# The RWKV scan: group norm of y moved to ScalarE, VectorE's order in a chunk changed, the samples' columns loaded first

## The chip, the cores and the metric

The program runs on one core of a Trainium2 chip (trn2). The metric is the device time of one execution in microseconds (us), lower is better. The kernel before takes 2999.13 us (median of 3 runs, 2998.64 to 3001.56). All data is fp32.

## What is computed

The whole program is one inference step of a 2-layer decoder trunk: an RWKV-7 layer and an attention layer, each followed by a squared-ReLU MLP, for one prompt of 1024 tokens and 8 samples of one token. The change lies in the RWKV-7 mixer, in its recurrence and in the norm of its output:

```python
def wkv7_step(state, inp):
    r_t, w_t, k_t, v_t, a_t, b_t = inp
    sa = jnp.einsum('bhij,bhj->bhi', state, a_t)
    state = (state * w_t[:, :, None, :] + sa[..., None] * b_t[:, :, None, :]
             + v_t[..., None] * k_t[:, :, None, :])
    y = jnp.einsum('bhij,bhj->bhi', state, r_t)
    return state, y
...
    state, y = lax.scan(wkv7_step, wkv_prev.astype(f32), xs)
    y = jnp.moveaxis(y, 0, 1)
    mu = jnp.mean(y, axis=-1, keepdims=True)
    var = jnp.mean(jnp.square(y - mu), axis=-1, keepdims=True)
    y = ((y - mu) * lax.rsqrt(var + LNX_EPS) * lnx_g.astype(f32).reshape(H, N)
         + lnx_b.astype(f32).reshape(H, N))
```

There are 16 heads of 64 channels. The mean and the variance are taken over the 64 channels of a head, for each token. The prompt starts from a zero state; the 8 samples have one step each, from a given state.

## The kernel before

The program is a row of stages, and between them all engines meet. The scan (`stage_scan`) follows the stage that makes its inputs (`stage_kvr`) and stands in front of the output projection with `rw_wo`. It handles the prompt in 16 chunks (NCH) of 64 tokens (C). Within a chunk the recurrence is a set of small matrix products, each made for 8 pairs of heads (DB = 8 blocks of 128 channels). Four chunks are one body of the loop (BODY = 4); the last four are written out.

One chunk, with the names of the PSUM tiles (the profile calls pSA c_pA):

- TensorE: `pU` takes 8 pairs of matmuls with the state S and 8 with the values V (the latter need the masked grams G). Then half of the grams of the next chunk into pB and pK, `pSA` from U, `pD` and `pY` with V and S, a wait for SA, then `pD` (the change of the state) and `pY` (the output), the other half of the next chunk's grams, and in `turn` four transposes of the y of three chunks ago (Y_LAG = 3) into pT.
- VectorE and ScalarE each copy one half of U, and one half of SA, out of PSUM into block-diagonal tiles. VectorE also masks the grams (`masked`, two halves, each two operations) and sums S from pD and the decayed state Sd.
- GpSimd makes the diagonal of the next chunk's decays (`diagonal`), which the grams need, and Sd, the decayed state.
- The norm of y runs beside it, some chunks late. Before the change: VectorE reduces y to sums and scales them (`mean`), GpSimd subtracts the mean and squares, VectorE reduces the squares (`variance`), ScalarE takes the root (`root`), VectorE the reciprocal (`inverse`), GpSimd multiplies y by it (`normalise`).
- VectorE works besides on the 8 samples (`Samples.step`): nine operations a chunk on 128x256 elements, in three parts of three, L2326 to L2328, L2329 to L2331 and L2332 to L2334. All but the two reduces read two tensors in SBUF. Their inputs come as columns (`Samples.load`), are turned by TensorE (`turn`) and evicted by ScalarE (`spread`), written to memory and loaded again by rows; the samples' state of 2 MB is loaded behind that.

The order on each engine is written out by hand, in `work(c, k, i, last)` of each engine's block; semaphores tie the engines together. VectorE's order in a chunk before is: copy of U, `inverse`, sample part 0, masks of half 0 for the next chunk, copy of SA, sample part 1, `variance`, sum into S, sample part 2, `mean`, masks of half 1.

Of the kernel before, what the change touches and what calls it, by code (L numbers as in the profile page):

```python
# [22 lines left out]
HD = 64  # L23
# [3 lines left out]
Y_LAG = 3  # L27
# [2356 lines left out]
def stage_scan(net):  # L2384
# [15 lines left out]
    with ExitStack() as ctx:  # L2400
# [16 lines left out]
        ym, yv, yi = (sb(n, [128, Q * 2]) for n in ("ym", "yv", "yi"))  # L2417
# [10 lines left out]
        s_ym, s_yc, s_ysq, s_yv, s_yr, s_yi, s_yn = sem("ym"), sem("yc"), sem("ysq"), sem("yv"), sem("yr"), sem("yi"), sem("yn")  # L2428
# [28 lines left out]
        each = lambda x: x.unsqueeze(2).to_broadcast([128, Q * 2, HD])  # L2457
# [39 lines left out]
        @block.gpsimd  # L2497
        def _(pool):
            pool.memset(BK[:, 0, 0], 0.0).then_inc(s_zeroP, 1)
            pool.memset(BK[:, 1], 0.0).then_inc(s_zeroP, 1)  # L2500
            pool.wait_ge(s_eye, 2)

            def work(c, k, i, last):
                s, cc = k // 2, k % 2
                decay = net.pend[:, :, bass.ds(c, 1)]
                pool.wait_ge(s_S, c + 1)
                pool.wait_ge(s_D, c + 1)
                if not last:
                    diagonal(c + 1, (k + 1) % BODY)
                pool.tensor_tensor(Sd[:], S[:], decay.to_broadcast([128, DB, 128]), ALU.mult).then_inc(s_dS, 1)  # L2510
                normalise(c, k)

            def normalise(c, k, full=True):
                y = heads(Y[:, (k - 3) % BODY])
                pool.wait_ge(s_yi, c + 1)
                pool.tensor_tensor(y, y, each(yi[:]), ALU.mult).then_inc(s_yn, 1)
                if not full:
                    return
                y = heads(Y[:, (k - 1) % BODY])
                pool.wait_ge(s_ym, c + 1)  # L2520
# [12 lines left out]
            for k in range(Y_LAG):  # L2533
                normalise(NCH + k, k, k == 0)

        @block.tensor
        def _(pe):
# [54 lines left out]
            def turn(c, k):  # L2592
                pe.wait_ge(s_yn, c + 2)
# [27 lines left out]
        def _(act):  # L2621
            for s in range(2):
                smp.load(act, (2 * s, 2 * s + 1))
                act.wait_ge(s_zeroV, s + 1)
                values(act, s, s)
            smp.spread(act, (pT, pY, pU, pSA, pD))

            def work(c, k, i, last):
# [3 lines left out]
                ins.then_inc(s_Ua, 1)  # L2632
                act.wait_ge(s_SA, c + 1)
# [3 lines left out]
                root(c)  # L2637
# [18 lines left out]
            def root(c):  # L2656
                act.wait_ge(s_yv, c + 1)
                act.activation(yv[:], yv[:], ACT.Sqrt).then_inc(s_yr, 1)
# [10 lines left out]
            for k in range(Y_LAG):  # L2669
                if k < 2:  # L2670
                    root(NCH + k)
# [10 lines left out]
        def _(dve):  # L2682
# [9 lines left out]
            for n, buf in enumerate((Y, ysq, Yt)):  # L2692
                dve.memset(buf[:], 0.0).then_inc(s_ydv, 1)
            dve.memset(yv[:], 1.0).then_inc(s_ydv, 1)
# [6 lines left out]
            for x in (s_yc, s_ysq, s_yn, s_yr, s_yTe, smp.s_dv, s_Yev, s_Ua, s_Ud, s_Sa, s_Sd, s_D):  # L2701
# [8 lines left out]
            def work(c, k, i, last):  # L2710
# [5 lines left out]
                inverse(c)  # L2716
# [10 lines left out]
                smp.step(dve, c, 1)  # L2727
                variance(c)
# [11 lines left out]
            def mean(c, k, made, n=2):  # L2740
                dve.wait_ge(s_Yev, made + 1)
                dve.wait_ge(s_yc, c + 1)
                dve.tensor_reduce(ym[:], heads(Y[:, (k - 1) % BODY]), AX, ALU.add).then_inc(s_ydv, 1)
                dve.wait_ge(s_ydv, 4 + c * 2 + n)
                dve.tensor_scalar(ym[:], ym[:], 1.0 / HD, None, ALU.mult).then_inc(s_ym, 1)

            def variance(c, n=1):
                dve.wait_ge(s_ysq, c + 1)
                dve.tensor_reduce(yv[:], ysq[:], AX, ALU.add).then_inc(s_ydv, 1)
                dve.wait_ge(s_ydv, 4 + c * 2 + n)  # L2750
                dve.tensor_scalar(yv[:], yv[:], 1.0 / HD, LNX_EPS, ALU.mult, ALU.add).then_inc(s_yv, 1)

            def inverse(c):
# [7 lines left out]
            for k in range(Y_LAG):  # L2761
                inverse(NCH + k)
                if k == 0:
                    mean(NCH, 0, NCH, 1)
                if k < 2:
                    dve.wait_ge(s_yi, NCH + k + 1)
                    variance(NCH + k, 2 - k)
# [514 lines left out]
```

## Time and profile before

| | us |
|---|---|
| median of 3 runs | 2999.13 |
| profiled execution | 2994.69 |
| its span | 2992.9 |
| PE busy in the span | 2689.9 |
| DVE busy | 1277.1 |
| ACT busy | 944.0 |
| POOL busy | 590.9 |

PE is TensorE, PEld its weight loads, DVE VectorE, ACT ScalarE, POOL GpSimd, SP SyncE. A row of the timeline tells the start in us, the duration, the engine, the line, what is written from what, the shape, and in brackets how long the engine stood idle before it and what ended that. PEclk is the clock granted to TensorE as a share of its full 2.4 GHz, so 0.50 is 1.2 GHz. Over the whole program PE is the busiest engine; within the scan this is a matter of its own, which the rows show.

### The profile page before, as it was taken

To read this page: it belongs to the slowest core of one execution; us is meant where nothing else is said; L and a number is where in the kernel's file an instruction comes from. 1 tells how busy PE (TensorE), PEld (TensorE's weight loads), DVE (VectorE), ACT (ScalarE), POOL (GpSimd) and SP (SyncE) were. 2 spreads that over 40 slices of the span, in tenths; PEclk is the share of its full clock that TensorE was granted. 3 is DMA by queue.
4 is the path that set the end of the run, shared out by engine and by line. 5 is a ranking of instruction groups with operands and counts; after the bars stand their busy time and mean duration, and the time that the engine had idled before them with its cause. 6 is when DMAs were issued, how large, how long until landed. Compare 5 with 4: busy or idle time off the path is not lost. (4 is left out here: it accounts for less than half of the span.)

```text
span 2992.9 us, 46796 instructions
## 1 busy us (share of the span) xinstructions
PE 2689.9 (90%) x19528; PEld 2531.1 (85%) x19528; DVE 1277.1 (43%) x2250; ACT 944.0 (32%) x1809; POOL 590.9 (20%) x357
## 2 busy tenths in 40 slices
PE   4879878958886899999999999898899999999998
PEld 3648768947775789999999999777799999999998
DVE  5236776338886742121121235466563222121223
ACT  4337623312213442121120234356543122131221
POOL 1011111113344002112112230210201222221230
PEclk7989989989997899999999999999999999999999
DMA  8866659684465412222222231411111111111121
GB/s 317 305 225 205 207 183 272 202 183 106 101 139 192 130 50 86 92 71 85 92 85 85 71 97 53 121 28 47 55 60 36 50 44 49 50 43 50 49 65 57
DMA packets 379486, 331.87 MB, mean 111 GB/s; under 512 B 109863, under 2 KB 349163, under 8 KB 372221
## 3 DMA queue, kind: packets, MB, share of 16 engines
q1 hardware_dynamic: 349180, 287.17, 32.1%
q10 hardware_dynamic: 24384, 21.87, 2.5%
q0 software_dynamic: 5728, 20.06, 1.8%
q8 instruction: 145, 2.38, 0.3%
q14 instruction: 49, 0.39, 0.0%
HBM read 248.92 MB, written 78.78 MB: 109 GB/s over the span
## 5 line engine op out<-in xcount | busy, mean ns | idle before, releaser
L524 POOL TENSOR_TENSOR wL<-raw,wH 128x1024 fp32r<-128x1024 f32 x120 | 288.1, 2401 | 1297.0 <-ACT wH L648 1297.0
L545 PE MATMUL t_acc<-oneH,wH 128*128 128x344 f32 x1488 | 482.6, 324 | 12.3 <-DVE oneL L892 6.3
L547 PE MATMUL t_acc<-oneH,wL 128*128 128x344 f32 x1488 | 477.6, 321 | 0.0
L546 PE MATMUL t_acc<-oneL,wH 128*128 128x344 f32 x1488 | 477.2, 321 | 0.0
L545 PE MATMUL t_acc<-twoH,wH 128*128 128x344 f32 x1392 | 449.0, 323 | 7.0 <-DVE twoL L867 4.8
L547 PE MATMUL t_acc<-twoH,wL 128*128 128x344 f32 x1392 | 445.5, 320 | 0.0
L546 PE MATMUL t_acc<-twoL,wH 128*128 128x344 f32 x1392 | 445.1, 320 | 0.0
L817 DVE SCALAR_TENSOR_TENSOR X<-t_acc,mod,X 128x344 f32<-128x344 f32 (+1 forms) x240 | 137.4, 572 | 611.4 <-PE t_acc L547 590.2
L897 DVE TENSOR_TENSOR t_g<-t_g 128x344 f32<-128x344 f32 x192 | 99.3, 517 | 553.3 <-ACT t_g L668 553.3
L545 PEld LDWEIGHTS t_acc<-oneH,wH 128*128 128x128 f32 x1488 | 281.4, 189 | 26.4 <-issue 10.1
L648 ACT ACTIVATE wH<-raw 128x1024 fp32r<-128x1024 f32 x120 | 126.7, 1056 | 507.6 <-PE t_acc L547 507.6
L546 PEld LDWEIGHTS t_acc<-oneL,wH 128*128 128x128 f32 x1488 | 281.9, 189 | 0.6
L547 PEld LDWEIGHTS t_acc<-oneH,wL 128*128 128x128 f32 x1488 | 281.5, 189 | 0.0
L545 PEld LDWEIGHTS t_acc<-twoH,wH 128*128 128x128 f32 x1392 | 262.3, 188 | 20.1 <-issue 11.2
L546 PEld LDWEIGHTS t_acc<-twoL,wH 128*128 128x128 f32 x1392 | 262.6, 189 | 0.1
L547 PEld LDWEIGHTS t_acc<-twoH,wL 128*128 128x128 f32 x1392 | 262.3, 188 | 0.0
L668 ACT ACTIVATE t_g<-t_acc 128x344 f32<-128x344 f32 x192 | 87.7, 457 | 507.8 <-PE t_acc L547 507.8
L1962 PE MATMUL kvr_acc<-hxH,kvr_wH 128*128 128x344 f32 x480 | 161.8, 337 | 20.8 <-POOL kvr_wL L1844 17.5
L1963 PE MATMUL kvr_acc<-hxL,kvr_wH 128*128 128x344 f32 x480 | 156.1, 325 | 0.0
L1964 PE MATMUL kvr_acc<-hxH,kvr_wL 128*128 128x344 f32 x480 | 155.9, 325 | 0.0
L545 PE MATMUL t_acc<-twoH,oneH 128*128 128x344 f32 x336 | 113.5, 338 | 31.4 <-DVE twoL L892 30.7
L1844 POOL TENSOR_TENSOR kvr_wL<-kvr_wraw,kvr_wH 128x1024 fp32r<-128x1024 f32 x24 | 63.3, 2636 | 334.1 <-ACT kvr_wH L2000 334.1
(481 smaller groups left out, 5039.4 us busy)
## 6 DMA issues: line engine op xcount, KB each, us to landing
raw<-in_mlp_down SPq DMA_DIRECT2D x64, 512.0 KB, 3.8
raw<-in_mlp_up SPq DMA_DIRECT2D x62, 512.0 KB, 4.2
ada_ring<-in_ada_w SPq DMA_DIRECT2D x24, 1024.0 KB, 8.7
shared<-in_ada_w SPq DMA_DIRECT2D x24, 1024.0 KB, 6.2
kvrb_hx<-hx_saved ACTq DMA_DIRECT2D x16, 516.5 KB, 3.7
kvr_work<-scr_L SPq DMA_DIRECT2D x16, 516.0 KB, 5.1
X<-x_saved SPq DMA_DIRECT2D x6, 1376.0 KB, 7.5
raw<-in_at_wqkv SPq DMA_DIRECT2D x12, 512.0 KB, 4.0
```

What stands on the lines that cost most here:

```text
L524: pool.tensor_tensor(low, raw_of(w), high.bitcast(F32), ALU.subtract).then_inc(s_low, 1)
L545: pe.matmul(out, high[:, k, :], h[:, k, third[t]], start=(k == 0), stop=False)
L546: pe.matmul(out, high[:, k, :], l[:, k, third[t]], start=False, stop=False)
L547: return pe.matmul(out, low[:, k, :], h[:, k, third[t]], start=False, stop=(k == DB - 1))
L648: act.activation(place(kind, p)[0], raw_of(w), ACT.Copy).then_inc(s_high, 1)
L668: act.activation(gsq[:, i % 3, :], acc[u % 4][:, 0:TT], ACT.Relu).then_inc(s_relu, 1)
L817: ins = dve.scalar_tensor_tensor(out=x, in0=acc[u % 4][:, 0:z - a], scalar=gate[:, m, 0:1], in1=x, op0=ALU.mult, op1=ALU.add)
L897: dve.tensor_tensor(x, x, x, ALU.mult).then_inc(s_g, 1)
L1844: pool.tensor_tensor(wL[:, p % 2], raw[:, p % 2], wH[:, p % 2].bitcast(F32), ALU.subtract).then_inc(s_low, 1)
L1962: pe.matmul(out, wH[:, s, b, :], net.HH[:, b, t], start=(b == 0), stop=False)
L1963: pe.matmul(out, wH[:, s, b, :], net.HL[:, b, t], start=False, stop=False)
L1964: ins = pe.matmul(out, wL[:, s, b, :], net.HH[:, b, t], start=False, stop=(b == DB - 1))
```

## The change

Three things.

The norm of y leaves GpSimd. ScalarE squares y less its mean by heads, eight instructions of 128x64 with an accumulated sum (`squares`), and scales by heads, eight of 128x64 with a scale and a bias per partition (`normalise`). VectorE loses the reduce of the squares and gains one product of 128x8 (`nm`). ym and yv get a place per chunk of the body.

VectorE's order in a chunk becomes: copy of U, sample part 0, copy of SA, `variance`, masks of half 0, `inverse`, sum into S, sample part 1, `mean`, masks of half 1, sample part 2.

ScalarE issues all four loads of the samples' columns, and the samples' values, in front of its loads of V.

```diff
@@ gpsimd @@
                 pool.tensor_tensor(Sd[:], S[:], decay.to_broadcast([128, DB, 128]), ALU.mult).then_inc(s_dS, 1)
-                normalise(c, k)
-
-            def normalise(c, k, full=True):
-                y = heads(Y[:, (k - 3) % BODY])
-                pool.wait_ge(s_yi, c + 1)
-                pool.tensor_tensor(y, y, each(yi[:]), ALU.mult).then_inc(s_yn, 1)
-                if not full:
-                    return
-                y = heads(Y[:, (k - 1) % BODY])
-                pool.wait_ge(s_ym, c + 1)
-                pool.tensor_tensor(y, y, each(ym[:]), ALU.subtract).then_inc(s_yc, 1)
-                pool.wait_ge(s_yc, c + 2)
-                pool.wait_ge(s_yv, c + 1)
-                pool.tensor_tensor(ysq[:], y, y, ALU.mult).then_inc(s_ysq, 1)
...
@@ tensor @@
             def turn(c, k):
-                pe.wait_ge(s_yn, c + 2)
+                pe.wait_ge(s_yn, c + 1)
...
@@ scalar @@
+            smp.load(act, range(4))
             for s in range(2):
-                smp.load(act, (2 * s, 2 * s + 1))
                 act.wait_ge(s_zeroV, s + 1)
                 values(act, s, s)
...
                 ins.then_inc(s_Ua, 1)
+                squares(c, k)
                 act.wait_ge(s_SA, c + 1)
                 for o, p in halves(0, SA, pSA):
                     ins = act.activation(o, p, ACT.Copy)
                 ins.then_inc(s_Sa, 1)
-                root(c)
+                root(c, k)
+                normalise(c, k)
                 act.wait_ge(s_Y, c + 1 + Y0)
                 act.activation(Y[:, k], pY[:], ACT.Copy).then_inc(s_Yev, 1)
                 turned(c, k, i)
...
+            def squares(c, k):
+
+                y = heads(Y[:, (k - 2) % BODY])
+                act.wait_ge(s_ym, c + 1)
+                act.wait_ge(s_ysq, c + 1)
+                for g in range(2 * Q):
+                    ins = act.activation(ysq[:, g, :], y[:, g, :], ACT.Square, bias=ym[:, (k - 1) % BODY, g:g + 1], accum_out=yv[:, k % BODY, g:g + 1])
+                ins.then_inc(s_ysq, 1)
+
+            def root(c, k):
                 act.wait_ge(s_yv, c + 1)
-                act.activation(yv[:], yv[:], ACT.Sqrt).then_inc(s_yr, 1)
+                act.activation(yv[:, k % BODY], yv[:, k % BODY], ACT.Sqrt).then_inc(s_yr, 1)
+
+            def normalise(c, k):
+                y = heads(Y[:, (k - 2) % BODY])
+                act.wait_ge(s_nm, c + 1)
+                for g in range(2 * Q):
+                    ins = act.activation(y[:, g, :], y[:, g, :], ACT.Identity, bias=nm[:, g:g + 1], scale=yi[:, g:g + 1])
+                ins.then_inc(s_yn, 1)
...
             for k in range(Y_LAG):
                 if k < 2:
-                    root(NCH + k)
+                    squares(NCH + k, k)
+                    root(NCH + k, k)
+                    normalise(NCH + k, k)
...
@@ vector @@
                 ins.then_inc(s_Ud, 1)
-                inverse(c)
                 dve.wait_ge(smp.s_S, 16)
                 dve.wait_ge(smp.s_vec, 96)
                 smp.step(dve, c, 0)
-                if not last:
-                    dve.wait_ge(s_Y, c + Y0)
-                    masked(c + 1, 1 - g, 0)
                 dve.wait_ge(s_SA, c + 1)
                 for o, p in halves(1, SA, pSA):
                     ins = dve.tensor_copy(o, p)
                 ins.then_inc(s_Sd, 1)
-                smp.step(dve, c, 1)
-                variance(c)
+                variance(c, k)
+                if not last:
+                    dve.wait_ge(s_Y, c + Y0)
+                    masked(c + 1, 1 - g, 0)
+                inverse(c, k)
                 dve.wait_ge(s_D, c + 2)
                 dve.wait_ge(s_dS, c + 1)
...
                 ins.then_inc(s_S, 1)
-                smp.step(dve, c, 2)
-                mean(c, k, c)
+                smp.step(dve, c, 1)
+                mean(c, k)
                 if not last:
                     masked(c + 1, 1 - g, 1)
...
+                smp.step(dve, c, 2)
+
+            def mean(c, k):
+                dve.wait_ge(s_Yev, c + 1)
+                dve.tensor_reduce(ym[:, k % BODY], heads(Y[:, (k - 1) % BODY]), AX, ALU.add).then_inc(s_ydv, 1)
+                dve.wait_ge(s_ydv, c + 5)
+                dve.tensor_scalar(ym[:, k % BODY], ym[:, k % BODY], -1.0 / HD, None, ALU.mult).then_inc(s_ym, 1)
+
+            def variance(c, k):
+                dve.wait_ge(s_ysq, c + 2)
+                dve.tensor_scalar(yv[:, k % BODY], yv[:, k % BODY], 1.0 / HD, LNX_EPS, ALU.mult, ALU.add).then_inc(s_yv, 1)
+
+            def inverse(c, k):
                 dve.wait_ge(s_yr, c + 1)
                 dve.wait_ge(s_yn, c + 1)
-                dve.reciprocal(yi[:], yv[:]).then_inc(s_yi, 1)
+                dve.reciprocal(yi[:], yv[:, k % BODY]).then_inc(s_yi, 1)
+                dve.wait_ge(s_yi, c + 1)
+                dve.tensor_tensor(nm[:], ym[:, (k - 1) % BODY], yi[:], ALU.mult).then_inc(s_nm, 1)
```

## Rows read from the trace of the kernel before

**Rows 1.** Busy time by windows, one stretch of the chunk loop: engine's busy us (instructions), clock, DMA.
```profile
720.00:904.00 184.00, 152.48 (x1932) 137.66 (x1930) 163.49 (x308) 39.27 (x86) 69.23 (x57) 1.00 0.55 118
```

**Rows 2.** Timeline of one chunk, VectorE.
```profile
744.27 0.68 DVE L2743 TENSOR_REDUCE c_ym<-c_Y 128x8 f32<-128x512 f32 x1
...
747.94 0.87 DVE L2714 COPY c_U<-c_pU 64x256 f32<-64x256 f32 x2 [1.20 <-PE c_pU L2540]
...
748.95 1.60 DVE L2326 TENSOR_TENSOR step_t<-step_S,step_vec 128x256 f32<-128x256 f32 x1
...
750.48 1.26 DVE L2327 TENSOR_TENSOR step_t<-step_vec 128x256 f32<-128x256 f32 x1
...
753.81 0.87 DVE L2725 COPY c_SA<-c_pA 64x256 f32<-64x256 f32 x2
...
756.89 1.73 DVE L2733 TENSOR_TENSOR c_S<-c_pD,c_Sd 64x256 f32<-64x256 f32 x4
```

**Rows 3.** The same timeline, TensorE, and ScalarE's copy of SA.
```profile
744.71 1.09 PE L2540 MATMUL c_pU<-c_S,c_ARI 128*64 128x128 f32 x16
...
746.79 1.09 PE L2540 MATMUL c_pU<-c_V,c_G 128*64 128x128 f32 x16 [0.99 <-DVE c_G L2708]
...
748.54 0.48 PE L2551 MATMUL c_pB<-c_ARI,c_BK 128*128 128x128 f32 x2 [0.65 <-POOL c_ARI L2528]
...
750.92 1.09 PE L2540 MATMUL c_pA<-c_U,c_Z 128*64 128x128 f32 x16
...
752.06 0.76 ACT L2635 ACTIVATE c_SA<-c_pA 64x256 f32<-64x256 f32 x2 [3.37 <-PE c_pA L2540]
...
754.83 1.09 PE L2540 MATMUL c_pD<-c_SA,c_G 128*64 128x128 f32 x16 [1.07 <-DVE c_SA L2725]
...
760.45 1.09 PE L2540 MATMUL c_pU<-c_S,c_ARI 128*64 128x128 f32 x16
```

**Rows 4.** The same timeline, GpSimd.
```profile
747.35 1.06 POOL L2528 TENSOR_TENSOR c_ARI<-c_eye,pend 128x512 f32<-128x512 f32 x1
...
748.36 1.91 POOL L2510 TENSOR_TENSOR c_Sd<-c_S,pend 128x1024 f32<-128x1024 f32 x1
...
750.23 1.23 POOL L2516 TENSOR_TENSOR c_Y<-c_Y,c_yi 128x512 f32<-128x512 f32 x1
```

**Rows 5.** Instructions by tile: duration ns min/median/max, first and last start.
```profile
L2329 DVE TENSOR_TENSOR step_S<-step_S,step_t x16: 424/426/426, 675.6 to 909.1; 128x256 f32 x12, 128x256 f32<-128x256 f32 x4
L2751 DVE TENSOR_SCALAR c_yv<-c_yv x18: 171/171/393, 677.6 to 922.8; 128x8 f32<-128x8 f32 x18
```

**Rows 6.** ScalarE: an accumulating one (attention, timeline), one with two pointers (groups).
```profile
1928.79 0.39 ACT L3110 ACTIVATE a_S<-a_S,a_nm 128x129 f32<-128x129 f32 x1
...
L683 ACT ACTIVATE shared<-shared,mod,gain 128x344 f32<-128x344 f32 x48 | 31.8, 663 | 15.5 <-DVE shared L852 15.5
```

**Rows 7.** Busy time by windows around two falls of the clock, and one PE row.
```profile
902.50:906.00 3.50, 1.59 (x26) 1.11 (x22) 2.26 (x5) 0.86 (x3) 3.42 (x3) 1.00 0.52 150
906.00:909.00 3.00, 2.96 (x28) 2.99 (x30) 2.95 (x6) 0.75 (x2) 1.54 (x2) 0.50 0.03 8
1026.50:1030.00 3.50, 0.23 (x2) 0.00 (x0) 3.46 (x6) 3.17 (x7) 0.80 (x1) 0.84 0.00 0
1030.00:1034.00 4.00, 2.33 (x7) 1.89 (x8) 2.74 (x6) 1.63 (x4) 0.00 (x0) 0.50 0.47 121
...
906.04 1.97 PE L2540 MATMUL c_pA<-c_U,c_Z 128*64 128x128 f32 x16 [1.06 <-DVE c_U L2714]
```

**Rows 8.** Timeline at the stage's head: first use of the columns and of the samples' state.
```profile
646.42 1.02 PE L2301 MATMUL c_pT<-const,step_cols 128*8 128x128 f32 x4 [21.51 <-DMA step_cols<-scr_Kt]
...
671.90 0.42 DVE L2326 TENSOR_TENSOR step_t<-step_S,step_vec 128x256 f32<-128x256 f32 x1 [7.81 <-DMA step_S<-in_state_wkv]
```

**Rows 9.** Timeline at the stage's end: issue of the prompt's state, last eviction of Yt.
```profile
915.40 2.17 ACTq L2668 DMA_DIRECT2D out_wkv_prompt<-c_St  x2
...
926.29 0.60 ACT L2651 ACTIVATE c_Yt<-c_pT 128x512 f32<-128x512 f32 x1 [0.99 <-PE c_pT L2596]
```

More of the change, by code:

```diff
@@ L2416, in stage_scan @@
         ysq = sb("ysq", [128, Q * 2, HD])
-        ym, yv, yi = (sb(n, [128, Q * 2]) for n in ("ym", "yv", "yi"))
+        ym, yv = (sb(n, [128, BODY, Q * 2]) for n in ("ym", "yv"))
+        yi, nm = (sb(n, [128, Q * 2]) for n in ("yi", "nm"))
         Yt = sb("Yt", [128, 2, DB, 2, C])
@@ L2427, in stage_scan @@
         s_dec, s_dS, s_eye = sem("dec"), sem("dS"), sem("eye")
-        s_ym, s_yc, s_ysq, s_yv, s_yr, s_yi, s_yn = sem("ym"), sem("yc"), sem("ysq"), sem("yv"), sem("yr"), sem("yi"), sem("yn")
+        s_ym, s_ysq, s_yv, s_yr, s_yi, s_nm, s_yn = sem("ym"), sem("ysq"), sem("yv"), sem("yr"), sem("yi"), sem("nm"), sem("yn")
         s_yT, s_yTe, s_ydv, s_yz = sem("yT"), sem("yTe"), sem("ydv"), sem("yz")
@@ L2456, in stage_scan @@
         heads = lambda y: y.rearrange("p q (a d) -> p (q a) d", a=2)
-        each = lambda x: x.unsqueeze(2).to_broadcast([128, Q * 2, HD])
         @block.sync
@@ L2532, in _ @@
             chunks(pool, work)
-            for k in range(Y_LAG):
-                normalise(NCH + k, k, k == 0)
         @block.tensor
@@ L2654, in turned @@
                     act.dma_start(net.sYc[:, :, bass.ds(c * C, 2 * C)].rearrange("b p t -> p b t"), Yt[:, slot].rearrange("p b c t -> p b (c t)")).then_inc(s_yst[slot], 16)
-            def root(c):
-                act.wait_ge(s_yv, c + 1)
-                act.activation(yv[:], yv[:], ACT.Sqrt).then_inc(s_yr, 1)
+            def squares(c, k):
[6 more added lines that the diff above has]
+            def root(c, k):
+                act.wait_ge(s_yv, c + 1)
+                act.activation(yv[:, k % BODY], yv[:, k % BODY], ACT.Sqrt).then_inc(s_yr, 1)
[5 more added lines that the diff above has]
+                ins.then_inc(s_yn, 1)
             act.wait_ge(s_yz, 1)
@@ L2691, in _ @@
                 dve.tensor_copy(eye[r], ident[r, r]).then_inc(s_eye, 1)
-            for n, buf in enumerate((Y, ysq, Yt)):
+            for buf in (Y, Yt, ym, yv):
                 dve.memset(buf[:], 0.0).then_inc(s_ydv, 1)
-            dve.memset(yv[:], 1.0).then_inc(s_ydv, 1)
             dve.wait_ge(s_ydv, 4)
@@ L2700, in _ @@
             dve.sem_inc(s_yst[1], 16)
-            for x in (s_yc, s_ysq, s_yn, s_yr, s_yTe, smp.s_dv, s_Yev, s_Ua, s_Ud, s_Sa, s_Sd, s_D):
+            for x in (s_ym, s_ysq, s_yn, s_yTe, smp.s_dv, s_Yev, s_Ua, s_Ud, s_Sa, s_Sd, s_D):
                 dve.sem_inc(x, 1)
@@ L2734, in work @@
                 ins.then_inc(s_S, 1)
-                smp.step(dve, c, 2)
-                mean(c, k, c)
+                smp.step(dve, c, 1)
+                mean(c, k)
                 if not last:
                     masked(c + 1, 1 - g, 1)
[L2740 to L2753, printed above, removed]
+                smp.step(dve, c, 2)
[8 more added lines that the diff above has]
+            def inverse(c, k):
                 dve.wait_ge(s_yr, c + 1)
                 dve.wait_ge(s_yn, c + 1)
-                dve.reciprocal(yi[:], yv[:]).then_inc(s_yi, 1)
+                dve.reciprocal(yi[:], yv[:, k % BODY]).then_inc(s_yi, 1)
+                dve.wait_ge(s_yi, c + 1)
+                dve.tensor_tensor(nm[:], ym[:, (k - 1) % BODY], yi[:], ALU.mult).then_inc(s_nm, 1)
             for half in range(2):
@@ L2760, in _ @@
             chunks(dve, work)
[L2761 to L2767, printed above, removed]
+            mean(NCH, 0)
+            for k in range(2):
+                variance(NCH + k, k)
+                inverse(NCH + k, k)
                 if k == 0:
```

## Prediction, made before the changed kernel was run

> **What bounds the kernel now.** I read the page first for the stage: the scan's sixteen chunks lie at about 660 to 914 us of the span. The view by windows comes next [rows 1]: over 184 us of the chunk loop VectorE (DVE) is busy 163.49 us, TensorE (PE) 152.48, GpSimd (POOL) 69.23 and ScalarE (ACT) 39.27, at a granted clock of 1.00, TensorE's upper level (2.4 GHz). The timeline of one chunk then shows who waits. The same matmuls onto pU start at 744.71 and 760.45 [rows 3], so a chunk takes 15.74 us. DVE stands idle for 1.20 us of that, before its copy of U [rows 2]. PE waits three times in a chunk: 0.99 us for DVE's masked grams, 0.65 for POOL's diagonal, 1.07 for DVE's copy of SA [rows 3]. DVE's order is the bound. Two things in it are waste. The copy of SA starts at 753.81 although ACT could start its half at 752.06, because the masks of the next chunk stand in front. And the first two sample steps take 1.60 and 1.26 us beside two POOL instructions that last over the same time [rows 2, 4], where the same form of instruction takes 0.43 us [rows 5]: each ends some 0.28 us after POOL's ends (748.36 + 1.91 = 750.27, against 750.55). So a DVE operation on two SBUF tensors stands still while a POOL one runs. That is 2.0 us in each chunk.
>
> **What the change does to a chunk, step by step.** I count from u, the start of the second group onto pU (746.79), which waits for the masks.
> Removed: POOL's three passes over Y, and with them POOL's lateness. POOL's diagonal and Sd no longer stand behind the mean, so PE's 0.65 goes. DVE loses a reduce of 128x512 (0.68, as the mean's) and gains one product of 128x8, 0.20 as the scalar operations with their gaps.
> Step a: from u, PE does its group, the grams and pA; SA could be copied at 752.06 - 746.79 - 0.65 = 4.6 us. By then DVE has done the third sample part, its copy of U and the first part, all undisturbed since POOL has long finished: 1.35 + 0.9 + 1.35 = 3.6 us. DVE waits there, 1.0 us.
> Step b: copy of SA 0.90 [rows 2], variance 0.20, masks of half 0, 1.6 (from the mean's start to pU it is 746.79 - 744.27 = 2.52, less the mean's 0.91 with its scalar operation), inverse with its product 0.45, sum into S 1.75 [rows 2]. PE's own work from the start of pA to the second group onto pD is 2.7 us without its wait (754.83 - 1.07 - 750.92 = 2.84, of which some is the tail of the last matmul). That makes pD start at u + 6.1 and end 1.1 later, before the sum into S at u + 7.7; it isn't late.
> Step c: the sum into S frees POOL at the same moment as it frees DVE's next part, which is now the second sample part: three products or sums on two SBUF tensors, each waiting for the last. POOL does diagonal (1.06) and Sd (1.91) at once [rows 4]. Counted from the end of that sum: the first DVE one gets through (0.43), the diagonal, started 0.1 to 0.3 behind, ends at about 1.33, the second ends at 1.61, Sd, delayed as the 1.23 us one in [rows 4], ends at 3.4, the third at 3.7. Undisturbed they would take 1.35. Even were they let through, the mean's scalar operation is stopped as well: one took 0.39 at the end of the stage, beside a pass of POOL's, 0.17 being usual [rows 5].
> Step d: mean and masks of half 1, 2.52, and the next u.
> Sum: 4.6 + 0.9 + 0.2 + 1.6 + 0.45 + 1.75 + 3.7 + 2.5 = 15.7 us. The chunk is as long as before. The 1.75 us won at SA, the 0.5 of the reduce and the 2.0 of contention come back as 2.35 of contention in front of the masks and as DVE's wait for SA.
> The masks of half 0 move behind the copy of SA; the grams of half 1, which wait for them, start 2.8 us after pD, the masks end 1.1 after it, so they hide. The wait for the root stands in front of the sum into S: ACT does the short root beside the masks of 1.6 us, and a table load in every fourth chunk fits there too. Were that cover gone it would cost up to the masks' 1.6 us in 4 of 16 chunks.
>
> **ScalarE.** It gets 8 squares with an accumulator and 8 scalings per chunk. The nearest row of the first kind is 128x129 in 0.39 us with its read [rows 6], these are 128x64; so 2.7 to 3.1 us per chunk. ACT is free from u + 1.9 (after its copy of U) and has to start on SA by 5.2, that is 3.3 us: they hide, by 0.2 to 0.6 us. The scalings, below 0.66 [rows 6] and I take 0.35 (280 columns fewer), are 2.8 us from u + 7.7, and Y's eviction behind them has until the next chunk. Nothing there is on the chain. Their price if squares cost 0.5 each is 0.7 us per chunk (11 us), kept for the range.
>
> **TensorE's clock.** PE ends its first group onto pU 6.7 us after pD's start (760.45 - 754.83 + 1.1) and waits for u at 15.7 - 6.1 = 9.6: 2.9 us idle in one piece in each chunk. Before, the pieces were 0.99, 0.65 and 1.07. The windows of [rows 7] show two falls: PE was busy for 0.23 of 3.5 us and the clock behind it was 0.50 (1.2 GHz); and in the last chunk it was busy for 1.59 of 3.5 us, in pieces with idles near 1 us between, and the 3 us after 906.0 had 0.50. There 16 matmuls took 1.97 us against 1.09. The first matmuls after the new idle piece are all on the chain (pU, grams, pA). A fall as the one at 906 lost 0.88 us on each of two groups, 1.7 in all, if it lies wholly behind the idle piece, and less where it begins in it. It need not come in each chunk: bounds 0 and 1.7 per chunk. I take 1.3, since the piece is nearer to the one of over 3 us that fell than to the 1.0 ones that didn't. Over 14 chunks + 18.2 us.
>
> **Ends of the stage.** Head: PE waited until 646.42 for the last of the samples' columns, and DVE 7.81 us for the samples' state, to 671.90 [rows 8]. ACT's loads now come in one row without its wait for the cleared V, so the columns land by about 640, and ACT's spread (held by its own issuing) starts 4 to 8 us earlier. The 2 MB state behind it shares the DMA engines, which are full there, with the other loads: I take 3 of these. In chunk 0 the copy of SA no longer follows the masks, 1.6, but the sample parts collide after it: 0.9 net. Together -3.7 (bounds -8 and 0).
> Tail: from the end of ACT's issue of the prompt's state (915.40 + 2.17) to the end of the last eviction of Yt (926.29 + 0.60) it took 9.3 us [rows 9], with the passes over Y on POOL. Now ACT does in that place twice 8 squares, root, wait for DVE and 8 scalings, 2 x (2.8 + 0.65 + 0.5 + 2.7) = 13.3, and 2.6 for the samples' root and columns, two evictions and the last transposes: 15.9. In front of it the last chunk's scalings hold Y's last eviction by 0.6. So +7.2 (bounds +4, +9). The stage behind starts only when these evictions have landed.
> Loop: 14 x (15.70 - 15.74) = -0.6.
> Sum: -3.7 + 7.2 - 0.6 + 18.2 = +21.1 us. On the profiled execution's 2994.7 us (span 2992.9 and 1.8 around it) that is 3015.8. That execution is 4.4 us under the median 2999.13 of the runs; the difference goes onto the median: **3020 us**.
>
> The Trainium skill (SBUF — State Buffer, Who interferes with whom) states what [rows 2, 4] show, that a DVE instruction with two SBUF inputs and a GpSimd one that reads SBUF exclude each other for a whole instruction. It speaks against this order: by it step 1 is put exactly where POOL starts. The sum above would be the same without it.
>
> **Rivals.**
> The clock holds: the idle piece of 2.9 us is shorter than the one of over 3 us behind which a row shows a fall, and the loop's own three pieces never brought one. Then +2.9: 3002 us. The Trainium skill (TensorE: Matmul & The Clock Gate, HAM oscillation — how this bites in real kernels) has falls begin with longer idle pieces than mine; by that rule this is the outcome. The fall at 906, after much shorter ones, speaks against it. Chance 0.17.
> The collision is smaller: POOL comes to its diagonal late enough, or loses to DVE each time. If only the scalar operation of the mean is stopped, a chunk is 15.7 - 1.2 = 14.5 us, the idle piece 1.7 and the clock mostly holds: -17.4 + 3.5, 2985 us. If nothing is stopped it is 15.7 - 2.35 = 13.35 us, and 14 x (13.35 - 15.74) + 3.5 = -30, 2969 us. For it: POOL's start behind a release is not shown for this pair. Against it: [rows 4], where POOL's instruction took the port ahead of a DVE one already issued. Chance 0.22.
> The clock's fall stretches: if it stays low through the whole of grams, pA and pD, up to 3 us per chunk, or the squares delay SA as well: +35 to +45, 3040 us. It decides where PE isn't busy enough in the low stretch to come back. Chance 0.11.
> My forecast has 0.50.
>
> **Numbers.** Differences under 0.2% (6 us) can't be told from no change. Slower: forecast and the stretched fall, 0.61, and a little of the rival at 3002: 0.63. Same: 0.15. Faster: 0.22. The range leaves out the undisturbed case and the far end: 2983 to 3036. The likeliest case's own range, with its bounds of clock and ends, is 3006 to 3031.
>
> **What would show it.** In the new profile: the second sample part's three instructions at 0.4, 1.2 and 2.0 us beside POOL's Sd; the copy of SA at once behind pA; PE idle 2.9 us before the second group onto pU, released by the last mask; granted clock about 0.85 to 0.9 over the loop; the chunk at 17 us; the last eviction of Yt some 16 us behind the issue of the prompt's state. Wrong it is if the masks of half 1 come less than 2 us after the sum into S, or if the clock stays at 1.00.

## The result, and the profile after

The changed kernel takes 3015.79 us (median of 5 runs, 3012.45 to 3023.66), the kernel before 2999.13 (5 runs, 2998.64 to 3001.56). The ratio is 1.0059, 95% interval 1.0043 to 1.0075: slower by 0.6%, by more than the runs' noise. The forecast was 3020 us.

| | before | after |
|---|---|---|
| median of 5 runs | 2999.13 | 3015.79 |
| profiled execution | 2994.69 | 3014.17 |
| its span | 2992.9 | 3012.3 |
| one chunk in the loop | 15.74 | 16.94 |
| PE / DVE / ACT / POOL busy in the span | 2689.9 / 1277.1 / 944.0 / 590.9 | 2712.1 / 1267.3 / 1040.8 / 540.5 |

The page of the kernel after, its first lines:

```profile
span 3012.3 us, 47136 instructions
## 1 busy us (share of the span) xinstructions
PE 2712.1 (90%) x19528; PEld 2554.3 (85%) x19528; DVE 1267.3 (42%) x2249; ACT 1040.8 (35%) x2241; POOL 540.5 (18%) x304
```

PE does the same 19528 matmuls in 22.2 us more: they did not grow, their clock fell. The view by windows of the kernel after, the stretch of [rows 1] (columns as there: PE, PEld, DVE, ACT, POOL busy, granted clock, DMA share, GB/s):

```profile
720.00:904.00 184.00, 156.07 (x1780) 144.65 (x1777) 149.37 (x286) 95.51 (x341) 35.51 (x22) 0.90 0.53 117
```

POOL went from 69.23 to 35.51 us and ACT from 39.27 to 95.51. DVE is down from 163.49 to 149.37, for the most part because the stretch holds fewer chunks: 163.49 us in 184 / 15.74 chunks are 14.0 us in each, 149.37 in 184 / 16.94 are 13.8. The granted clock was 1.00 and is 0.90. The timeline of one chunk after, its chain and what stands beside it:

```profile
747.47 1.40 PE L2524 MATMUL c_pU<-c_V,c_G 128*64 128x128 f32 x16 [2.54 <-DVE c_G L2711]
748.81 0.80 PE L2535 MATMUL c_pB<-c_ARI,c_BK 128*128 128x128 f32 x2
...
752.05 0.33 ACT L2648 ACTIVATE c_ysq<-c_Y,c_ym 128x64 f32<-128x64 f32 x1
...
752.50 1.09 PE L2524 MATMUL c_pA<-c_U,c_Z 128*64 128x128 f32 x16
...
753.64 0.76 ACT L2620 ACTIVATE c_SA<-c_pA 64x256 f32<-64x256 f32 x2 [1.17 <-PE c_pA L2524]
753.64 0.87 DVE L2724 COPY c_SA<-c_pA 64x256 f32<-64x256 f32 x2 [2.60 <-PE c_pA L2524]
...
756.53 1.72 DVE L2735 TENSOR_TENSOR c_S<-c_pD,c_Sd 64x256 f32<-64x256 f32 x4
756.64 2.76 ACT L2659 ACTIVATE c_Y<-c_Y,c_nm,c_yi 128x64 f32<-128x64 f32 x8 [1.69 <-DVE c_nm L2758]
...
758.28 0.43 DVE L2329 TENSOR_TENSOR step_S<-step_S,step_t 128x256 f32 x1
758.50 1.13 POOL L2514 TENSOR_TENSOR c_ARI<-c_eye,pend 128x512 f32<-128x512 f32 x1 [13.75 <-DVE c_S L2735]
...
758.75 1.17 DVE L2330 TENSOR_TENSOR step_t<-step_sa,step_vec 128x256 f32<-128x256 f32 x1
...
759.60 2.09 POOL L2510 TENSOR_TENSOR c_Sd<-c_S,pend 128x1024 f32<-128x1024 f32 x1
...
759.94 2.02 DVE L2331 TENSOR_TENSOR step_S<-step_S,step_t 128x256 f32 x1
...
761.89 0.67 DVE L2745 TENSOR_REDUCE c_ym<-c_Y 128x8 f32<-128x512 f32 x1
...
764.41 0.77 PE L2524 MATMUL c_pU<-c_V,c_G 128*64 128x128 f32 x10 [2.54 <-DVE c_G L2711]
```

The same matmuls start at 747.47 and at 764.41, 16.94 us apart. Three things are to be seen. The sum into S ends and lets go two engines at once: DVE's sample part 1 and POOL's diagonal with Sd. Three DVE instructions that take 0.4 us when left alone take 0.43, 1.17 and 2.02 beside them. PE runs out of work before the masks come and stands for 2.54 us. Behind that idle piece its matmuls are slow (1.40 us for the group onto pU, 0.80 for a pair of grams that takes 0.38 at the full clock), until pA is back at 1.09. So it is from the third chunk (696.67) to the fifteenth (900.12), 13 in all; in front of the second chunk PE stood even longer, and no fall followed:

```profile
681.36 1.09 PE L2524 MATMUL c_pU<-c_V,c_G 128*64 128x128 f32 x16 [3.03 <-DVE c_G L2711]
```

The granted clock from there to 684.90 was 1.00, and that chunk took 15.31 us (681.36 to 696.67).

Head and tail of the stage, from the same timeline: the spread of the samples' rows and the first sample step, and the end of the stage with the first instruction behind it:

```profile
645.98 0.59 ACT L2309 ACTIVATE step_rows<-c_pT 8x512 f32<-8x512 f32 x1 [35.24 <-PE c_pA L2301]
...
669.48 0.43 DVE L2326 TENSOR_TENSOR step_t<-step_S,step_vec 128x256 f32<-128x256 f32 x1 [5.15 <-DMA step_S<-in_state_wkv]
...
927.98 1.40 ACTq L2670 DMA_DIRECT2D out_wkv_prompt<-c_St  x2
...
933.15 2.76 ACT L2659 ACTIVATE c_Y<-c_Y,c_nm,c_yi 128x64 f32<-128x64 f32 x8 [0.47 <-DVE c_nm L2758]
...
940.68 2.76 ACT L2659 ACTIVATE c_Y<-c_Y,c_nm,c_yi 128x64 f32<-128x64 f32 x8 [0.47 <-DVE c_nm L2758]
...
945.25 0.60 ACT L2637 ACTIVATE c_Yt<-c_pT 128x512 f32<-128x512 f32 x1 [0.98 <-PE c_pT L2580]
...
950.30 1.06 ACT L648 ACTIVATE oneH<-raw 128x1024 fp32r<-128x1024 f32 x1 [4.46 <-PEq L122]
```

So the span's +19.4 us divide: the stage starts 0.7 later; from there to the second chunk's copy of U it takes 52.3 instead of 56.5 (-4.2); the fourteen chunks after that take 234.9 instead of 218.8 (+16.1); the issue of the prompt's state is 0.8 shorter (1.40 against 2.17, [rows 9]); from its end to the end of the last eviction it takes 16.5 instead of 9.3 (+7.2); the stages behind take 0.4 more.

### The profile page after: what moved, and what is told of

Same layout as the page of the kernel before. It is cut to its first block and busy times, and to the rows that moved or that the text cites. A ratio compares the mean times of both kernels' runs of the same rounds, so it can differ in the third digit from the quotient of the medians.

```text
span 3012.3 us, 47136 instructions
## 1 busy us (share of the span) xinstructions
PE 2712.1 (90%) x19528; PEld 2554.3 (85%) x19528; DVE 1267.3 (42%) x2249; ACT 1040.8 (35%) x2241; POOL 540.5 (18%) x304
```

## Experiments

The theory: a chunk is DVE's chain, with a collision in front of the masks that costs 2.35 us, and the idle piece of PE which that makes brings a fall of TensorE's clock. The rivals: the clock falls for another reason and costs nothing on the chain; the collision is not what sets the chunk; the norm's ACT work does. Where several ran together, they share the runs of the kernel before.

### The idle piece filled: e1_refill2 and e2_refill1

The changed kernel, whose first group onto pU is done three times in a row (e1) or twice (e2). The result is the same numbers, and nothing on DVE, ACT or POOL changes.

```diff
-                for b in range(DB):
-                    mm(pU, b, ARI[:, s, b, 0, cc, :], S[:, b, :], b < 2, False)
+                for again in range(3):
+                    for b in range(DB):
+                        mm(pU, b, ARI[:, s, b, 0, cc, :], S[:, b, :], b < 2, False)
```

> The changed kernel, with the first group of matmuls onto pU (8 pairs from S) made three times in a row instead of once; each time starts the sums anew, so the result is the same and only TensorE's idle piece in front of the second group is filled, by 2 x 0.88 of its 2.54 us. Theory (the fall of the clock after that piece costs 1.1 to 1.3 us per chunk): the granted clock stays at 1.00 over the loop, a chunk takes 15.7 us instead of 16.94, the whole 3000 us. Rival (the clock's fall lies beside other waits and costs nothing): clock 1.00 too, but chunk and time as in the changed kernel, 3016 us. Second rival (more work for TensorE on its own path): slower than 3016.

> The same with the group made twice: one more group of 0.88 us, so an idle piece of 1.7 us is left. [...] Rival (the fall comes with any single piece over 1.2 us): it falls as in the changed kernel, chunk near 16.9 us less nothing, 3014 us.

e1 took 2995.39 us, ratio to before 0.9995 (0.9985 to 1.0005), and e2 2996.46, 0.9998 (0.9984 to 1.0011): 512 and 256 matmuls more, and some 20 us less than the kernel without them. The view by windows and the timeline of e1:

```profile
720.00:900.00 180.00, 170.64 (x2316) 158.82 (x2312) 160.67 (x308) 100.53 (x360) 37.69 (x23) 1.00 0.55 123
```

```profile
750.45 0.87 DVE L2725 COPY c_SA<-c_pA 64x256 f32<-64x256 f32 x2 [1.12 <-PE c_pA L2524]
750.49 0.75 ACT L2621 ACTIVATE c_SA<-c_pA 64x256 f32<-64x256 f32 x2
...
755.55 1.16 DVE L2330 TENSOR_TENSOR step_t<-step_sa,step_vec 128x256 f32<-128x256 f32 x1
...
757.57 2.84 PE L2524 MATMUL c_pU<-c_S,c_ARI 128*64 128x128 f32 x48
...
761.21 1.09 PE L2524 MATMUL c_pU<-c_V,c_G 128*64 128x128 f32 x16 [0.79 <-DVE c_G L2712]
```

The same row of e2:

```profile
763.30 1.09 PE L2524 MATMUL c_pU<-c_V,c_G 128*64 128x128 f32 x16 [1.67 <-DVE c_G L2712]
```

Both times are near the 3000 us that were expected if the clock held. In both profiles the clock is 1.00 over the loop and a chunk takes 15.32 us, with the collision unchanged (1.16 us). So the fall costs 16.94 - 15.32 = 1.62 us a chunk, and it hangs on PE's idle piece: with 0.79 and with 1.67 us left of it there is none. The other 15.32 us are DVE's chain, 0.42 less than before the change. The 13 chunks with a fall make 13 x 1.62 = 21.1 us, and the whole stage is 22.3 us shorter in e1's profile (297.6 against 319.9): more than all that the change lost.

### The collision moved: e3_pool_late

The changed kernel; POOL waits for the masks of half 1 before it makes the diagonal and Sd.

```diff
                 pool.wait_ge(s_D, c + 1)
+                pool.wait_ge(s_Gev, c * 4 + 6)
```

> The changed kernel with one more wait on GpSimd: its diagonal and Sd begin only when the masks of half 1 are made. Theory (the collision of the second sample part with POOL lies on the chain, 2.35 us, and makes the idle piece that brings the clock down): the three sample operations take 0.43 us each, the chunk 13.4 us, clock 1.00, PE idle before the second group onto pU 0.6 us; 14 x (13.4 - 16.8) = -47, so 2969 us. Rival (the collision is beside the chain, DVE's amount of work is the limit): chunk unchanged or longer by POOL's lateness, 3016 us or more. Half way: the collision only moves to the third part and the first part, which then delay the copies of U and SA: 2985 us.

It took 2968.86 us, 0.9903 (0.9884 to 0.9922). Its timeline:

```profile
740.33 0.48 PE L2536 MATMUL c_pB<-c_ARI,c_BK 128*128 128x128 f32 x2 [0.28 <-POOL c_ARI L2515]
...
741.41 1.12 DVE L2326 TENSOR_TENSOR step_t<-step_S,step_vec 128x256 f32<-128x256 f32 x1
...
748.50 0.43 DVE L2329 TENSOR_TENSOR step_S<-step_S,step_t 128x256 f32 x1
...
748.96 0.42 DVE L2330 TENSOR_TENSOR step_t<-step_sa,step_vec 128x256 f32<-128x256 f32 x1
...
749.42 0.43 DVE L2331 TENSOR_TENSOR step_S<-step_S,step_t 128x256 f32 x1
...
749.76 0.68 DVE L2746 TENSOR_REDUCE c_ym<-c_Y 128x8 f32<-128x512 f32 x1
...
752.29 1.09 PE L2525 MATMUL c_pU<-c_V,c_G 128*64 128x128 f32 x16 [0.21 <-DVE c_G L2712]
```

Sample part 1 takes 0.4 us an instruction again. The collision now lies in the last operation of part 2 (0.66) and in part 0 (1.12), where DVE would wait for pA anyway, and the idle piece is down to 0.21 us. A chunk takes 13.33 us, 1.99 less than in e1: that is what taking the collision off the chain gives, and with the fall it makes 3.61 us a chunk. The stage took 270.2 us instead of 319.9, 49.7 less. One wait more on the engine with the most time made the kernel 47 us faster than the changed one. ACT's squares and scalings are all still there, so the norm's work on ACT is not what sets the changed kernel's chunk.

### One part alone: e6_norm_only, e9_order_only, e5_loads

e6 is the changed kernel, loads in front included, with DVE's order of before:

```diff
                 smp.step(dve, c, 0)
+                if not last:
+                    dve.wait_ge(s_Y, c + Y0)
+                    masked(c + 1, 1 - g, 0)
                 dve.wait_ge(s_SA, c + 1)
...
                 ins.then_inc(s_Sd, 1)
+                smp.step(dve, c, 1)
                 variance(c, k)
-                if not last:
-                    dve.wait_ge(s_Y, c + Y0)
-                    masked(c + 1, 1 - g, 0)
                 inverse(c, k)
...
                 ins.then_inc(s_S, 1)
-                smp.step(dve, c, 1)
+                smp.step(dve, c, 2)
                 mean(c, k)
                 if not last:
                     masked(c + 1, 1 - g, 1)
-                smp.step(dve, c, 2)
```

> The changed kernel with VectorE's order of before: copy of U, part 0, masks of half 0, copy of SA, part 1, variance, inverse, sum into S, part 2, mean, masks of half 1. So the norm is on ScalarE, the order is not changed. Theory (POOL, freed of the norm, starts right behind the sum into S and stops what VectorE has there in any order: here the third operation of part 2 and the mean's scaling): 15.2 us of chain per chunk with an idle piece of 2.4 us on TensorE, so with falls of the clock in most chunks 16 to 16.5 us, about 3008 us in all (3000 where the clock holds). Rival (the order is at fault, the norm's move is a gain by itself: 0.5 us less on DVE and no collision in part 0): 13.2 us per chunk, 2972 us.

It took 3013.37 us, 1.0056 (1.0042 to 1.007), as slow as the whole change. Its timeline and three windows of equal length that begin with the second group onto pU:

```profile
748.38 2.09 POOL L2510 TENSOR_TENSOR c_Sd<-c_S,pend 128x1024 f32<-128x1024 f32 x1
...
749.32 1.17 DVE L2747 TENSOR_SCALAR c_ym<-c_ym 128x8 f32<-128x8 f32 x1
...
752.13 1.09 PE L2524 MATMUL c_pU<-c_V,c_G 128*64 128x128 f32 x16 [2.13 <-DVE c_G L2711]
...
767.10 1.40 PE L2524 MATMUL c_pU<-c_V,c_G 128*64 128x128 f32 x16 [2.13 <-DVE c_G L2711]
```

```profile
718.90:722.40 3.50, 3.50 (x26) 3.33 (x26) 2.03 (x5) 2.34 (x12) 0.00 (x0) 0.65 0.12 32
735.50:739.00 3.50, 3.49 (x27) 3.32 (x28) 2.04 (x5) 2.31 (x11) 0.00 (x0) 0.72 1.36 208
752.10:755.60 3.50, 3.47 (x34) 3.07 (x34) 2.04 (x5) 2.29 (x11) 0.00 (x0) 1.00 0.13 35
```

Here the mean's scaling of 128x8 elements, 0.17 us alone, stands beside Sd for 1.17. PE's idle piece is 2.13 us in every chunk of the loop; behind it the clock fell in most chunks (0.65, 0.72 above) and held in others (1.00). From one second group onto pU to the next a chunk takes 16.6 us where it fell and 15.0 where it held (752.13 to 767.10 is 14.97). That is the price of the fall once more, 1.6 us a chunk, within one execution and with nothing added. It also shows that the chain became 0.8 us shorter than before (15.74): what loses is the clock. Moving the norm to ACT is enough for that; DVE's new order is not needed.

e9 is the kernel before, with the masks of half 0 moved behind the copy of SA and nothing else:

```diff
                 smp.step(dve, c, 0)
-                if not last:
-                    dve.wait_ge(s_Y, c + Y0)
-                    masked(c + 1, 1 - g, 0)
                 dve.wait_ge(s_SA, c + 1)
...
                 ins.then_inc(s_Sd, 1)
+                if not last:
+                    dve.wait_ge(s_Y, c + Y0)
+                    masked(c + 1, 1 - g, 0)
                 smp.step(dve, c, 1)
```

> The kernel before with one thing moved: the masks of half 0 stand behind VectorE's copy of SA instead of in front; the norm stays on POOL, the loads as before. Theory (VectorE's whole work, with what POOL stops in part 0, is the bound of the chunk, so a copy that comes 1.6 us earlier is paid back before the sum into S): the copy of SA starts 1.6 us earlier, TensorE's wait for it goes from 1.07 us to about 0, and the chunk stays at 15.7 us, 2996 to 2999 us. Rival (the copy of SA is on the chain and the masks are not): 1 to 1.6 us less per chunk, 2975 to 2982 us.

It took 3003.49 us against 2997.34 beside it, 1.0007 (0.999 to 1.0024), with runs from 2988.46 to 3012.28. The view by windows and the timeline:

```profile
720.00:900.00 180.00, 154.35 (x1782) 142.49 (x1780) 147.77 (x283) 35.14 (x79) 63.56 (x52) 0.91 0.56 120
```

```profile
716.41 1.09 PE L2540 MATMUL c_pU<-c_V,c_G 128*64 128x128 f32 x16 [1.84 <-DVE c_G L2708]
...
718.15 0.53 PE L2551 MATMUL c_pB<-c_ARI,c_BK 128*128 128x128 f32 x2 [0.65 <-POOL c_ARI L2528]
```

The copy of SA starts at once behind pA, as meant, and PE's 1.07 us wait there is gone. It comes back in front of the second group onto pU (1.84 us instead of 0.99), and POOL's 0.65 follows close behind. The pieces of before brought no fall in the stretch of [rows 1]; gathered into two they did, most chunks took 16.4 to 17.1 us, and the mean of the runs did not gain. That was not expected: the expectation had only the chain. One chunk of this profile's loop, from 801.45 to 816.90, kept the clock at 1.00 behind the same pieces and took 15.45 us, 0.3 less than before. The runs show the same two outcomes. The granted clock, as a mean over the whole program, was 0.956 or 0.957 in the four runs of 2988.46 to 2993.33 us and 0.948 to 0.953 in the eight of 3002.55 to 3012.28; the kernel before had 0.954 to 0.958 beside them. So the order by itself gives some 4 to 9 us in an execution in which the clock holds, and costs some 5 to 15 in one in which it falls. What makes it hold in one and fall in another stays open.

e5 is the kernel before, with the samples' columns loaded in front:

```diff
+            smp.load(act, range(4))
             for s in range(2):
-                smp.load(act, (2 * s, 2 * s + 1))
                 act.wait_ge(s_zeroV, s + 1)
```

> The kernel before with the third part of the change alone: the four loads of the samples' columns and the samples' values stand in front of the loads of V. Theory (the DMA engines are full at the head, so the samples' state lands only 2 to 3 us earlier, and that is what chunk 0 waits for): 2 to 3 us faster, 2996 us, first sample operation at about 669.5. Rival (the columns gate everything, the whole 4 to 8 us come through): 2992 us. Second rival (what was gained at the head in the changed kernel came from VectorE's order in chunk 0 alone): no change.

It took 2995.1 us against 2995.83 beside it, 0.9994 (0.9985 to 1.0003): by the runs, not to be told from no change. The timeline shows the gain where it should be:

```profile
673.58 0.43 DVE L2326 TENSOR_TENSOR step_t<-step_S,step_vec 128x256 f32<-128x256 f32 x1 [3.91 <-DMA step_S<-in_state_wkv]
```

That is 38.3 us behind the first load of the columns, before it was 42.2, after 39.1. That is 3.9 us earlier, of some 3000, at the edge of what the runs resolve. In the profiles the whole stage is 3.4 us shorter than before (298.2 against 301.6), although one chunk of this one took 16.20 us instead of 15.74: the clock fell in it, behind the same 1.00 and 0.65 us of idle time that every chunk has, and was 0.70 from 830.80 to 834.30.

### Further on: e4_order, e7_tail, e8_state

If the collision is the matter, DVE's own order can move it too, with nothing added on POOL. In e4 sample part 1 stands before the sum into S, and behind that sum come only operations that don't read two SBUF tensors, or can wait: the mean's reduce, the masks of half 1, and then the mean's scaling and sample part 2.

```diff
                 inverse(c, k)
+                smp.step(dve, c, 1)
                 dve.wait_ge(s_D, c + 2)
...
                 ins.then_inc(s_S, 1)
-                smp.step(dve, c, 1)
-                mean(c, k)
+                sums(c, k)
                 if not last:
                     masked(c + 1, 1 - g, 1)
+                mean(c, k)
                 smp.step(dve, c, 2)
```

`sums` is the reduce of `mean`, which keeps the scaling.

> The changed kernel with another order of VectorE and nothing else: second sample part in front of the sum into S (POOL idle then), behind the sum only the mean's reduce, which POOL doesn't stop, then the masks of half 1, then the mean's scaling and the third sample part. Theory: nothing that POOL can stop stands between the sum into S and the masks; the masks wait for TensorE's grams instead, chunk 13.1 us, clock 1.00, 2965 us. Rival (order is of no account, the collision follows wherever the sample parts go): chunk 15 us or more, 2990 to 3016 us.

It took 2961.78 us, 0.9881 (0.9862 to 0.99), a chunk 12.97. Its timeline:

```profile
747.96 0.81 DVE L2750 TENSOR_SCALAR c_ym<-c_ym 128x8 f32<-128x8 f32 x1
748.10 1.09 PE L2524 MATMUL c_pU<-c_V,c_G 128*64 128x128 f32 x16 [0.18 <-DVE c_G L2711]
...
752.65 0.87 DVE L2724 COPY c_SA<-c_pA 64x256 f32<-64x256 f32 x2 [0.39 <-PE c_pA L2524]
752.70 0.75 ACT L2620 ACTIVATE c_SA<-c_pA 64x256 f32<-64x256 f32 x2
```

The scaling is still stopped (0.81), but nothing waits for it. The masks come 0.18 us after PE is ready for them. Now PE stands idle only for those 0.18 us in a chunk, so the chunk is PE's, and the time that hid ACT's squares is used up: its copy of SA has no idle time in front of it and starts 0.05 behind DVE's, as soon as the squares are done.

e7 is e4 whose tail is divided (the edit is shown against e4, its part on DVE): of the two norms left after the last chunk, one is done by DVE over the full width (add the mean, square, reduce, later scale), the other by ACT as before. ACT takes both roots.

```diff
-            for k in range(2):
-                variance(NCH + k, k)
-                inverse(NCH + k, k)
...
+            dve.tensor_tensor(y, y, each(ym[:, 0]), ALU.add).then_inc(s_last, 1)
+            dve.tensor_tensor(sq, y, y, ALU.mult).then_inc(s_last, 1)
+            dve.tensor_reduce(var, sq, AX, ALU.add).then_inc(s_last, 1)
...
+            dve.tensor_tensor(y, y, each(var), ALU.mult).then_inc(s_yn, 1)
```

> The kernel with the mended order (second sample part before the sum into S, masks before the mean's scaling), and at the stage's end the last of the two left-over norms on VectorE, full width, beside ScalarE's of the other. Theory (the end got 7.2 us longer since ScalarE makes both norms one after the other, and the next stage waits for them): 6 to 7 us faster than the mended order alone, 2955 us. Rival (the loads of the next stage hide the end): as the mended order alone, 2962 us.

It took 2956.32 us, 0.9857 (0.984 to 0.9874). Its timeline:

```profile
877.37 1.43 ACTq L2670 DMA_DIRECT2D out_wkv_prompt<-c_St  x2
...
889.21 0.60 ACT L2637 ACTIVATE c_Yt<-c_pT 128x512 f32<-128x512 f32 x1 [0.98 <-PE c_pT L2580]
```

From the end of the issue to the end of the last eviction it takes 889.81 - 878.80 = 11.0 us instead of 16.5, which e4 has as well as the changed kernel. It was serial work on ACT that made the tail long. The intervals of e4 and e7 overlap; it is the stage in the profiles, 257.8 us against 263.9, that shows the gain.

e8 is e7 with the samples' state of 2 MB issued before the spread instead of behind it:

```diff
-        act.dma_start(self.S[:], self.net.io["state_wkv"][0].rearrange("s h i j -> (s h) i j")).then_inc(self.s_S, 16)
...
+            act.dma_start(smp.S[:], io["state_wkv"][0].rearrange("s h i j -> (s h) i j")).then_inc(smp.s_S, 16)
             smp.spread(act, (pT, pY, pU, pSA, pD))
```

> That kernel, and the samples' state of 2 MB is loaded by ScalarE in front of the eviction of the columns instead of behind their way through memory. Theory (chunk 0 waits 5 us for the state, the other loads aren't late): the first sample operation comes at once behind the copy of U, 3 to 5 us faster, 2951 us. Rival (the DMA engines are full, the state only displaces the loads that TensorE's first grams wait for): no change or slower, 2955 to 2960 us.

It took **2951.07 us** (2950.34 to 2951.78), 0.9849 (0.9833 to 0.9864), the lowest median of all (one of e7's four runs, 2947.17, lies under it). Its timeline:

```profile
672.04 0.42 DVE L2325 TENSOR_TENSOR step_t<-step_S,step_vec 128x256 f32<-128x256 f32 x1 [1.61 <-DMA step_vec<-scr_Smp]
```

The first sample step is 36.3 us behind the first load of the columns, and it waits for the vectors that went through memory, no longer for the state. e8 is 45 us (1.5%) under the kernel before that ran beside it (2995.83) and 65 under the changed one.

The stage's length in each profile, from the first load of the columns to the first instruction behind it, with the chunk in the loop and the granted clock of the window 720 to 900 us (worked out from starts as those above):

| | stage | chunk | clock |
|---|---|---|---|
| before | 301.6 | 15.74 | 1.00 |
| after | 319.9 | 16.94 | 0.91 |
| e1, e2 idle piece filled | 297.6, 297.0 | 15.32 | 1.00 |
| e6 norm and loads | 313.1 | 15.0 or 16.6 | 0.92 |
| e9 order alone | 312.6 | 15.45 or 16.4 to 17.1 | 0.91 |
| e5 loads alone | 298.2 | 15.74, one of 16.20 | 0.99 |
| e3 POOL late | 270.2 | 13.33 | 0.95 |
| e4 DVE order | 263.9 | 12.97 | 0.94 |
| e7 with divided tail | 257.8 | 12.97 | 0.94 |
| e8 with early state | 255.0 | 12.96 | 0.94 |

In the last four rows the window takes in the end of the stage, where the clock falls in any case (in e3 at 877 us); from 720 to 860 us it is 1.00 in all four.

## Why the prediction was right

**The chain.** The steps of the sum stand in the timelines one by one. From u to the copy of SA e1 has 4.56 us (said 4.6), copy 0.90 (0.9), variance to masks 0.20 (0.2), masks 1.47 (1.6), reciprocal with the product 0.31 (0.45), sum into S 1.76 (1.75), step c 3.60 (3.7), mean and masks 2.52 (2.5): 15.32 against 15.70. The 0.38 us too much are in the small terms. The largest are the masks, for which 1.6 was counted up to PE's start (in e1 too it is 1.61 from 759.60 to 761.21) where DVE's next instruction comes after 1.47, and the reciprocal with its product.

**The collision.** Forecast 0.4, 1.2 and 2.0 us for sample part 1, measured 0.43, 1.17 and 2.02: the pattern of [rows 2, 4] in a new place. The forecast read those rows as POOL going ahead of a DVE instruction already issued; they show only that the one that started first went first (POOL's at 750.23, DVE's at 750.48), and so it was here. Taking it away shortened step c from 3.60 to 1.26 us (748.50 to 749.76 in e3), 2.34 against the 2.35 of the sum; of a chunk it was worth 1.99 (e1 against e3), since in e3 the grams wait 0.28 for the late diagonal and SA is copied at u + 4.9. POOL came in 0.22 us behind DVE's first instruction. The rival "nothing is stopped" named 2969 us and a chunk of 13.35; e3, in which nothing is stopped on the chain, gave 2968.86 and 13.33. That rival's condition was wrong, POOL not coming late by itself, and that its price fits so well is in part luck: its chain was 0.38 too long, and e3, with POOL late, gained 1.99 where it took 2.35. The Trainium skill (SBUF — State Buffer, Who interferes with whom) says that a VectorE instruction with two inputs in SBUF and a GpSimd one that reads SBUF block each other for a whole instruction; the 1.17 and 2.02 us agree.

**The clock.** Forecast 1.3 us a chunk after an idle piece of 2.9, bounds 0 and 1.7. Measured 1.62 after 2.54, in 13 chunks, from the third to the fifteenth. The piece was shorter than forecast by just what the chain was too long. This term was mis-sized, by 0.3 us a chunk, and the 0.38 too much in the chain made up for it: 15.70 + 1.3 = 17.0 against 16.94. Two errors of opposite sign gave a chunk right to 0.06 us, and that is luck. The time is lost in the group onto pU and the grams (from 798 us on in the grams alone), while pA has its 1.09 us again; the size is near the upper bound, read off the fall at 906 us [rows 7]. That the fall would come was chosen by which of two rows lay nearer, not worked out; the 3.03 us in front of the second chunk, which brought none, show that the length of the piece does not decide alone. The rival that the clock holds (0.17) fell with the 0.90 over the loop; e1 and e2 show what a clock that holds gives, 2995 and 2996 us, and not 3002. The Trainium skill (TensorE: Matmul & The Clock Gate, HAM oscillation — how this bites in real kernels) has falls begin with longer idle pieces; the 2.54 us of the kernel after and the 2.13 of e6 disagree with that.

**ScalarE.** Said 2.7 to 3.1 us for the squares; they take 0.33 us each, 2.7 in all, and ACT then stands 1.17 us before its copy of SA: hidden, but only because pA comes 1.6 us later with the clock down. In e1, at the full clock, ACT's copy has no idle time in front of it and starts 0.04 us behind DVE's, and in e4 0.05: the margin of 0.2 to 0.6 us that the forecast gave is none. It had let ACT start on SA by u + 5.2, while its own step a had SA ready at u + 4.6; from u + 1.9 that leaves 2.7 us, just what the squares take. The scalings take 2.76 us (said 2.8).

**Head and tail.** Head: -3.7 forecast, -4.2 measured from the start of the stage to the second chunk, with the first sample step waiting 5.15 us for the state instead of 7.81. Two slips stand behind the forecast: its terms, 3 and 0.9, make 3.9 and not 3.7, and the spread, said to start 4 to 8 us earlier, came 2.2 earlier as counted from the stage's start (645.98 - 630.42 against 647.47 - 629.71, the first issues of the columns). Tail: 6.6 us more forecast between the two marks and 0.6 in front of them. Between the marks it was 7.2 more (16.5 us against the 15.9 of the sum), in front nothing: from the last copy of U to the issue it is 10.4 us in both kernels (917.58 to 927.98, before 905.03 to 915.40). So the +7.2 is met in the sum and not term by term. The issue in front was 0.8 us shorter, which nothing had foretold.

**The sum.** +21.1 forecast, +19.4 in the profiled spans, +16.7 between the medians. What lies between the first two: the fourteen chunks came out 1.15 us longer each, not 1.26 (-1.5; 13 of them had a fall, not 14), the head -0.5, the issue -0.8, the stage's start +0.7 and the stages behind +0.4. The rest is the spread of the runs: the changed kernel's reach from 3012.45 to 3023.66.

## What to carry to other kernels

Where an operation of one engine is released by the same event as an operation of another that stops it (here 0.43 us became 1.17 and 2.02), it is not enough to count each engine's busy time: here halving POOL's work in the loop moved POOL's remaining work to the worst moment, and a wait that made the idle engine later gained 47 us. Before gathering an engine's small waits into one by a better order, ask what TensorE's clock will do behind the longer one, and test it by filling the idle piece with repeated matmuls: if the kernel gets faster with more work, it was the clock. Check the terms of a forecast one by one, since a right sum does not show right terms: here a chain too long and a fall too cheap made one. And where the runs of one kernel spread, look at the granted clock of each run before calling it noise: e9's twelve runs fall into two groups by it.

## What the runs showed of the hardware that had not been expected

The granted clock fell behind idle pieces of PE of 2.54 us (after, 13 chunks, from the third to the fifteenth), of 2.13 us (e6, in most chunks, but not in those that start at 752.13, 816.95 and 865.12 us), behind 1.84 followed by 0.65 us (e9, but not in the chunk that starts at 801.45), and once in a loop behind 1.00 followed by 0.65 (e5, the chunk that starts at 827.30). It did not fall behind 3.03 us in front of the second chunk of the kernel after, nor in the profiled loops behind 1.67 (e2), 0.79 (e1), or the 0.99, 0.65 and 1.07 of the kernel before [rows 3]. The same idle piece in the same program does not always have the same effect, and its length alone does not tell which; what else decides stays open.

A DVE `tensor_scalar` over 128x8 elements, 0.17 us alone, took 1.17 us (e6) and 0.81 us (e4) beside GpSimd's product over 128x1024. The mean's reduce beside the same instruction kept its 0.67 us (e6).
